# Attention output projection and memory-cell values run by token block, values ahead of queries and keys, one conditioning panel moved from TensorE to VectorE

## What is computed

```python
# first block, its attention layer
o = ...                                   # attention output, (T, 1024)
x = x + (o * silu(gate)) @ w_out_b        # "wo_b"

# second block, first layer (memory cell, "mlstm")
cond = silu(c)
ada = cond @ ada_w[0] + ada_b[0]          # shift, scale, gate: six vectors of 1024
h = rmsnorm(x, norm_g[0, 0]) * (1 + sc1) + sh1
proj = h @ w_in                           # q (512), k (512), v (1024), i, f gates (8 + 8), output gate og (1024)
hh = mlstm_chunkwise(q, k, v, i_pre, f_pre)   # 8 heads
y = (rmsnorm(hh, head_g) * sigmoid(og)) @ w_out
x = x + g1 * rmsnorm(y, norm_g[0, 1])
```

## Time and profile before

| | us |
|---|---|
| median of 3 runs | 1046.74 |
| lowest and highest | 1046.15, 1050.27 |
| the profiled execution, whole time | 1047.87 |
| its span in the trace | 1046.10 |
| PE busy in it | 993.2 (95%) |
| DVE busy | 752.1 (72%) |
| ACT busy | 525.6 (50%) |

### The profile page before, as it was taken

One profiled execution on the slowest core, in us unless ns is written; L12 is line 12 of the kernel. 1 busy time (PEld: TensorE's weight loads), 2 busy tenths in 40 slices (PEclk: granted clock), 3 DMA queues, 4 the chain that ended last, 5 costly groups with the idle time before them and its releaser, 6 DMA issues.

```text
span 1046.1 us, 19356 instructions
## 1 busy us (share of the span) xinstructions
PE 993.2 (95%) x8274; PEld 864.8 (83%) x8274; DVE 752.1 (72%) x1277; ACT 525.6 (50%) x798; POOL 36.4 (3%) x33
## 2 busy tenths in 40 slices
PE   5999999968999999999999999999999899999996
PEld 4788899967788888788867899999688788999995
DVE  6789889577889958646589665676587895664544
ACT  3358431316454677455366445454466855445442
POOL 0000044200000100000000000000000000000000
PEclk9999999999999999999999999999999999999999
DMA  9674410492456550564264477776646444476411
GB/s 379 248 284 161 162 43 4 162 389 100 154 211 219 221 242 11 232 242 161 81 242 161 170 294 303 287 291 264 240 164 215 188 161 161 172 296 256 171 72 41
DMA packets 15222, 205.40 MB, mean 196 GB/s; under 512 B 1816, under 2 KB 1816, under 8 KB 2976
## 3 DMA queue, kind: packets, MB, share of 16 engines
q1 hardware_dynamic: 14544, 202.55, 50.5%
q10 hardware_dynamic: 592, 1.61, 0.5%
HBM read 203.10 MB, written 1.05 MB: 195 GB/s over the span
## 4 chain that ended last, share of the span: by engine, by line
PE 83%; DVE 10%; ACT 3%; issue 2%; DMA 1%; SPq 0%; DVEq 0%; ACTq 0%
PE bank L455 20%; PE bank L457 20%; PE bank L456 20%; PE bank L758 5%; PE bank L404 4%; DVE slot_parts L2019 2%; PE bank L661 1%; PE bank L562 1%; DMA ring<-in_stream 1%; PE bank L739 1%; PE bank L634 1%; DMA pc<-in_params 1%; PE bank L623 1%; PE bank L900 1%; PE bank L537 1%
## 5 line engine op out<-in xcount | busy, mean ns | idle before, releaser
L455 PE MATMUL bank<-page_parts 128*128 128x512 f32 (+3 forms) x1222 | 428.8, 351 | 6.8 <-DVE page_parts L2301 2.2
L2019 DVE TENSOR_TENSOR slot_parts<-ring,page_parts 128x2048 fp32r<-128x2048 f32 (+2 forms) x117 | 261.4, 2251 | 53.4 <-ACT page_parts L1356 52.9
L457 PE MATMUL bank<-page_parts 128*128 128x512 f32 (+2 forms) x750 | 291.4, 389 | 0.0
L456 PE MATMUL bank<-slot_parts,page_parts 128*128 128x512 f32 (+2 forms) x750 | 290.9, 388 | 0.0
L455 PEld LDWEIGHTS bank<-page_parts 128*128 128x128 f32 x1222 | 232.3, 190 | 36.5 <-issue 3.7
L1356 ACT ACTIVATE page_parts<-ring 128x2048 fp32r<-128x2048 f32 (+2 forms) x121 | 225.0, 1884 | 52.6 <-PE bank L457 28.1
L457 PEld LDWEIGHTS bank<-page_parts 128*128 128x128 f32 x750 | 141.3, 188 | 29.0
L456 PEld LDWEIGHTS bank<-slot_parts,page_parts 128*128 128x128 f32 x750 | 141.8, 189 | 26.8
L1434 ACT ACTIVATE arena<-bank 128x512 f32<-128x512 f32 (+2 forms) x134 | 74.2, 575 | 127.2 <-PE bank L457 67.0
L457 PE MATMUL bank<-page_parts,slot_parts 128*128 128x256 f32 x472 | 133.6, 283 | 0.0
L456 PE MATMUL bank<-page_parts 128*128 128x256 f32 x472 | 133.6, 283 | 0.0
(11 more groups left out here) (318 smaller groups left out, 1114.2 us busy)
## 6 DMA issues: line engine op xcount, KB each, us to landing
ring<-in_stream SPq DMA_DIRECT2D x95, 2048.0 KB, 8.0
arena<-in_x SPq DMA_DIRECT2D x2, 512.0 KB, 4.3
arena<-in_gn ACTq DMA_DIRECT2D x2, 512.0 KB, 4.4
out<-arena SPq DMA_DIRECT2D x2, 512.0 KB, 2.6
cc<-in_consts SPq DMA_DIRECT2D x1, 899.0 KB, 6.6
small<-in_cond ACTq DMA_DIRECT2D x1, 512.0 KB, 10.1
pc<-in_params SPq DMA_DIRECT2D x1, 287.0 KB, 6.8
arena<-in_head_sel ACTq DMA_DIRECT2D x1, 32.0 KB
```

What stands on the lines that cost most here:

```text
L455: mm(out, a[0], b[0], start=start, stop=False)
L456: mm(out, a[0], b[1], start=False, stop=False)
L457: return mm(out, a[1], b[0], start=False, stop=stop)
L2019: tt(unit_parts(n)[1], lo, hi, ALU.subtract).then_inc(dv.step("w_lo"), 1)
```

## The change: what it does

`wo_b` and `v2` are done by `split_blocks`: both halves of the output for token block 0, then both for block 1, with the four units kept until their use in block 1. The transposes of `hT_c` go by token block too, into `wo_b`'s block 1 and `v2`'s block 0 (`turn_block`). Order on PE is `wo_b`, `v2`, gates, `spread(0)`, `q2`, `k2`. The conditioning panel 12 is no longer multiplied on PE; it is reserved with panel 13 (`ada(2)`) behind `k2` and summed on DVE, and on DVE the modulation and diagonal of the first gate come ahead of the `v2` splits. The panel order is now 31, 32 `wo_b`; 33, 34 `v2`; 35 `q2`; 36 `k2`; 37, 38 conditioning; 39, 40 `og`. Units keep their pages by rotation: `wo_b` 28 to 31 on 15, 16, 3, 10; `v2` 32 to 35 on 6, 14, 1, 2; `q2` 36, 37 on 11, 15; `k2` 38, 39 again on 11, 15, because `from_first` is called anew for each panel; `og` 40 to 43 on 13, 15, 16, 8 as before.

```diff
 # PE
-            for half in range(2):
-                split_tok(("wo_b", half), split_parts(O1_PAGES), first_of(15, 16, 3), wait=("o1T_split", 0) if half == 0 else None)
+            def beside_wo_b(tb, n):
+
+                if (tb, n) == (1, 2):
+                    turn_block("hT_c", XN, 0, lambda g: (sem("xn"), 5))
+
+            def beside_v2(tb, n):
+
+                if (tb, n) == (0, 2):
+                    turn_block("hT_c", XN, 1, lambda g: (sem("xn"), 6))
...
+            split_blocks("wo_b", split_parts(O1_PAGES), from_first(15, 16, 3, 10), lambda tb, k: (sem("o1T_split"), k // 2 + 1), beside_wo_b)
...
-            ada_direct()
-            pe.wait_ge(sem("xn"), 6)
-            transposes("hT_c", XN)
-            ada_turned()
             stage[0] = "mlstm"
-            for name in ("q2", "k2"):
-                split_T((name,), split_parts(MLSTM_PAGES), first_of(6, 14, 11), wait=("hT_c_split", 0) if name == "q2" else None)
-                if name == "q2":
-                    ada(1)
+            split_blocks("v2", split_parts(MLSTM_PAGES), from_first(6, 14, 1, 2), lambda tb, k: (sem("hT_c_split"), 2 * tb + k // 4 + 1),
+                         beside_v2)
...
-            for half in range(2):
-                split_tok(("v2", half), split_parts(MLSTM_PAGES), first_of(6, 14, 11))
+            for name in ("q2", "k2"):
+                split_T((name,), split_parts(MLSTM_PAGES), from_first(11, 15, 16))
+            ada(2)
...
-            pe.wait_ge(*evacuated(("v2", 1, 1)))
+            pe.wait_ge(*evacuated(("k2", 1)))
 # ACT
-            split(unit_of["q2", 0] + 1)
+            split(unit_of["v2", 0] + 1)
             warm_root()
-            x_squares("wo_b")
-            ada_direct()
-            mod_scaled("hT_c", 0, hT2)
-            ada_turned()
...
+            for tb in range(TB):
+                x_block("wo_b", tb)
+                split(unit_of["v2", 0] + 2 + tb)
...
+            for tb in range(TB):
+                for half in range(2):
+                    copy(V2[:, tb, 4 * half:4 * half + 4, 0:DV], ("v2", half, tb))
...
+            for i in range(2):
+                split(ahead(("q2", i)))
+                pair([d[:, 2 * i:2 * i + 2, :] for d in Q2T_OF], ("q2", i))
+            act_.wait_ge(sem("m_total"), 1)
+            act(em_row[0:8, :], mt_row[0:8, :], ACT.Exp, scale=-1.0).then_inc(ac.step("gate_rows"), 1)
+            page_used.update({13: finished(("hT_c", 1, 1)), 8: finished("gates")})
+            copy(K2T[:, 0:2, :], ("k2", 0))
+            split(unit_of["og", 0] + 1)
+            copy(K2T[:, 2:4, :], ("k2", 1))
+            split(unit_of["og", 1] + 1)
 # DVE
             split_output("wo_b", "o1T", O1_PAGES)
-            split(unit_of["q2", 0] + 1)
-            add_to_x("wo_b")
...
+            modulation(4, 6, ())
+            gate_diagonal(0)
+            u = unit_of["v2", 0]
+            split(u + 1)
+            for tb in range(TB):
+                add_to_x("wo_b", (tb,))
+                for q in range(2):
+                    split_quarter(u + 2 + tb, q)
+                norm_block(tb)
+                for q in range(2, 4):
+                    split_quarter(u + 2 + tb, q)
+                split_rows("hT_c", MLSTM_PAGES, 0, tb)
+            for _ in range(4):
                 next_unit(("q2", 0))
...
+            ada(4)
             dve.wait_ge(sem("gate_ln"), 1)
...
             V.memset(V2[:, :, :, DV:DV + 1], 1.0).then_inc(dv.step(), 1)
-            next_unit(("q2", 0))
-            next_unit(("q2", 0))
             gate_row(0)
+            ada(4)
             split(unit_of["og", 1] + 1)
             dve.wait_ge(*finished("gate_cols"))
```

More of the change, by code:

```diff
@@ L976, in _, with from_first @@
             stage[0] = "wo_b"
-            for half in range(2):
-                split_tok(("wo_b", half), split_parts(O1_PAGES), first_of(15, 16, 3), wait=("o1T_split", 0) if half == 0 else None)
+            def beside_wo_b(tb, n):
[4 more added lines that the diff above has]
+                    turn_block("hT_c", XN, 1, lambda g: (sem("xn"), 6))
+            def from_first(*pages):
+                n = len(units) % len(pages)
+                return pages[-n:] + pages[:-n] if n else pages
+            split_blocks("wo_b", split_parts(O1_PAGES), from_first(15, 16, 3, 10), lambda tb, k: (sem("o1T_split"), k // 2 + 1), beside_wo_b)
             def spread(i):
@@ L987, in spread @@
                     ins.then_inc(filled(("gb", i, half)), 1)
-            def from_first(*pages):
-                n = len(units) % len(pages)
-                return pages[-n:] + pages[:-n] if n else pages
             def mlp(l, branch, src, wait, beside):
@@ L1705, in _ @@
             split(unit_of["wo_b", 1] + 1)
-            def mod_scaled(name, which, dst):
-                act_.wait_ge(sem("mod"), which + 1)
-                scaled(name, dst, MODS[which][0], MODS[which][1])
             def mlp(l, branch):
@@ L1785, in _ @@
             act_.dma_start(head_sel[0:8, :], sel_d).then_inc(sem("head_sel"), 16)
-            page_used.update({6: finished(("o1T", 3)), 14: finished(("at1", "O", 3)), 11: finished(("wo_b", 1, 1))})
-            split(unit_of["q2", 0] + 1)
+            page_used.update({6: finished(("o1T", 3)), 14: finished(("at1", "O", 3)), 1: finished(("at1", "O", 3)), 2: (sem("o1"), 2),
+                              11: finished(("wo_b", 1, 1))})
+            split(unit_of["v2", 0] + 1)
             warm_root()
-            x_squares("wo_b")
-            ada_direct()
-            mod_scaled("hT_c", 0, hT2)
-            ada_turned()
[L1793 to L1797, removed]
+            for tb in range(TB):
+                x_block("wo_b", tb)
+                split(unit_of["v2", 0] + 2 + tb)
+                p, (scale, bias) = ("hT_c", tb, 0), MODS[0]
+                act_.wait_ge(sem("mod"), 1)
+                act_.wait_ge(*finished(p))
+                for j in range(4):
+                    act(hT2[:, j, tb * P:(tb + 1) * P], bank(p)[:, j * P:(j + 1) * P], ACT.Identity, scale=scale[:, j:j + 1],
+                        bias=bias[:, j:j + 1]).then_inc(ac.frees(p) if j == 3 else ac.step(), 1)
+            for tb in range(TB):
+                for half in range(2):
+                    copy(V2[:, tb, 4 * half:4 * half + 4, 0:DV], ("v2", half, tb))
             gb = par("gate_b")
@@ L2516, in post_norm_block, with split_rows @@
                 dve.wait_ge(*dv.last)
-            def mlp(l, branch):
[L2520 to L2537, removed]
+            def split_rows(turned, pages, modulated, tb):
+                t = slice(tb * P, (tb + 1) * P)
+                hi, lo = split_parts(pages)
+                scale, bias = MODS[modulated]
+                p = (turned, tb, 1)
+                dve.wait_ge(*finished(p))
+                for j in range(4, 8):
+                    ts(hT2[:, j, t], bank(p)[:, (j - 4) * P:(j - 3) * P], scale[:, j:j + 1], bias[:, j:j + 1], ALU.mult,
+                       ALU.add).then_inc(dv.frees(p) if j == 7 else dv.step(), 1)
+                for g in range(2):
+                    js = slice(4 * g, 4 * g + 4)
+                    dve.wait_ge(*evacuated((turned, tb, g)))
+                    V.tensor_copy(hi[:, js, t], hT2[:, js, t]).then_inc(dv.step(), 1)
+                    dve.wait_ge(*dv.last)
+                    tt(lo[:, js, t], hT2[:, js, t], hi[:, js, t].bitcast(F32), ALU.subtract).then_inc(dv.step(turned + "_split"), 1)
+            def mlp(l, branch):
+                first, turned, modulated = unit_of["up", l, 0], f"hT_m{l}", (1, 4)[l]
                 def low_rows(e, n, tb):
@@ L2551, in mlp @@
                     split_quarter(first + 2, q)
-                split_rows(0)
+                split_rows(turned, MLP_PAGES, modulated, 0)
                 post_norm_block(2 * l, branch, 1)
@@ L2558, in mlp @@
                     split_quarter(first + 3, q)
-                split_rows(1)
+                split_rows(turned, MLP_PAGES, modulated, 1)
                 split(first + 4)
@@ L2581, in mlp @@
                     split(unit_of["cq"] + 1)
[L2584 to L2587, removed]
-                next_unit(("q2", 0))
[L2589 to L2593, removed]
+            modulation(4, 6, ())
[11 more added lines that the diff above has]
+            for _ in range(4):
+                next_unit(("q2", 0))
+            ada(4)
             dve.wait_ge(sem("gate_ln"), 1)
```

## The result

The changed kernel takes 1066.2 us (median; 1065.12 to 1070.58) against 1046.65 of the kernel before: 1.0186 times as long, interval 1.0169 to 1.0202, which is 17.7 to 21.1 us more. The prediction said 1065 and a sum of 18.4 us. Of these, 20.7 lie between the first matmul of `wo_b` and the first of `wo_c`, the projection behind the heads; the other 2.0 lie outside what the change touches.

What follows compares the result with a forecast made beforehand. PE was taken as the bound, with 83% of the chain. 14.8 + 0.4 + 3.2 = 18.4 us on the profiled 1047.87 gave 1066.3, so 1065 for the median; forecast's range 1060 to 1070, 8 in 10 from 1056 to 1071.

Steps and rivals of the forecast that it cites:

- The saving: From wo_b's start to v2's end: 80.6 us before, 74.4 for the same matmuls and transposes, 6.2 us saved if nothing waited.
- First seam, block 0: First transposes of hT_c, in wo_b: PE stands 5.65 us for the norm, as DVE waits for ACT's split of unit 34.
- First seam, block 1: Second transposes of hT_c, in v2: PE stands 1.75 us for block 1's norm.
- Second seam: Between k2 and the heads: og's first matmul waits for DVE's gate-column copy, which frees bank 7; 14.8 us later.
- The second limit: At og's start: panel 40 loads into k2's slot, then ACT and DVE splits and the copy follow, ending at 501.6.
- Behind the heads: At wo_c: it claims bank 1, which ACT frees with its second conditioning row, 0.4 us later than the row before.
- The clock: Behind the two new long PE waits the granted clock falls, costing 1.6 us each, 3.2 us in all.
- The bound of 2 x 1.7: Upper bound on the clock time lost behind the two new long PE waits; the lower bound was 0.
- the 1 us named as a sign: Sign to look for: k2 should end 1 us later than v2 did in the kernel before.
- the exception: At the kernel's start the clock was taken as 1.00 behind a wait of 11.72 us, against the idle-throttling rule.
- The 22.7 us of DVE's queue: Work put behind q2's end on DVE, cited against the case that nothing waits (1040.5 us, chance 0.07).
- a clock that doesn't fall: Case within the forecast: the clock stays up behind the new waits, 1062 us; a quarter of the forecast's chance of 0.78.

Runs made afterwards that it cites:

- the kernel with both seams mended: Changed kernel with the waits before the heads mended, ACT's v2 splits ahead of the squares, and modulation and diagonal behind both blocks; 1043.39 us, 0.9948 of the kernel before.
- the first experiment: Changed kernel with ACT's splits of v2's last two units put ahead of the squares; 1063.06 us, ratio 1.0145 to the kernel before.
- the second experiment: Changed kernel with DVE's copy of the gate columns ahead of the second conditioning sum and og splits; 1062.3 us, ratio 1.0127 to the kernel before.
- the third: Changed kernel with k2's units on pages 16 and 11 instead of 11 and 15; 1067.77 us, ratio 1.0189 to the kernel before.
- the run with the panel alone: Kernel before with only conditioning panel 12 summed on DVE instead of multiplied on PE, bank claims kept; 1048.4 us, ratio 1.0006.
- filled waits: Changed kernel with 66 overwritten matmuls added in PE's waits at the first transposes and before the heads; 1065.33 us, ratio 1.0167 to the kernel before.
- the kernel with the second seam mended: Changed kernel with k2's pages, DVE's scans, gate-column copy, og's splits and k2's copies reordered around the heads' start; 1053.28 us, ratio 1.0041 to the kernel before.

## Why the prediction was right

- **The saving.** Forecast 6.2 us if nothing waits; the kernel with both seams mended has 6.17 at the first `og` matmul, and as a whole 3.3 to 7.4.
- **First seam, block 0.** Forecast 5.65 us of wait; the trace has 5.15. Counted from `wo_b`'s start, which lies 0.5 us later in this trace than the 405.6 of the forecast, the adds were forecast done at 15.6 us and the first transposes at 22.05; the trace has 15.3 and 21.7. DVE's wait for ACT's split: forecast 3.4, measured 3.47. Shown to be the cause by the first experiment.
- **First seam, block 1.** Forecast 1.75, measured 1.71.
- **Second seam.** Forecast 14.8 us later at the first `og` matmul. Measured 17.3 (99.77 less 82.48), of which the clock behind the first seam is 2.9; 14.4 are left. The single waits are 1.20, 4.30 and 7.22 us, forecast 2.1 (487.45 to 489.5), 4.2 and 7.5; the first is shorter because ACT did the table load ahead of its wait for DVE's scans, at 482.27, where I had put its 1.28 us behind them. That the bank holds `og` is shown by the second experiment; that the panel's load is the next limit and a quicker DVE gains 1 us, by the third (0.84 in its trace). The second limit, 501.6, was worked out with a landing of 8.0 us, not with the median of 8.5 that I named, which gives 502.1; the trace has 8.2 (490.24 to 498.47).
- **Behind the heads.** Forecast 0.4 for the bank of the conditioning row; `wo_c` starts 20.7 us later than before and the first `num` 20.2, so 0.5. PE stands 0.82 us there in the two kernels with the old bank claims and 1.35 to 1.40 in every kernel with the new ones. That it is the conditioning row's bank rests on the count of claims: the profile names no engine for the longer wait.
- **The clock.** The one term that was too small. I took 1.6 us for each of two falls, by the row of a wait of 2.87 us (the row itself gives 1.7). In the profiled execution the clock was at half for 5.7 and 6.2 us of work behind the two waits (windows above), which is 2.9 and 3.1 us. It stayed at half for longer behind these waits than behind that short one. The bound of 2 x 1.7 that I gave was too low for this execution. The clock is also why `k2` ended 3.4 us later than `v2` had, counted from `wo_b`'s start, and not the 1 us named as a sign.
- **By the page.** The Trainium skill's rule ("TensorE: Matmul & The Clock Gate", Part 1), that an idle TensorE is throttled, was borne out at the waits of 5.15, 4.59 and 2.01 us in these traces. The start of the kernel, which the prediction took for the exception, is none. I read the printed 1.00 and not the durations: behind the 11.72 us idle, 16 transposes take 3.65 us, as the 16 at half clock in the run with the panel alone (3.67) and not as the 1.96 at full clock. The clock records of this trace begin only at 15.68 us, and the view prints 1.00 where it has none.
- **A slip without effect.** The 22.7 us of DVE's queue run from the end of unit 39's split (480.0), not from `q2`'s end (475.85).

The row of the start, from the timeline of PE in the kernel before:

```profile
11.72 3.65 PE L562 MATMUL bank<-cc,arena 128*128 128x128 f32 x16 [11.72 <-DVE arena L1961]
```

So the lower bound of 0 for the clock rested on a row that was misread, and with it the only reason that the text gives for the quarter of the chance put on a clock that doesn't fall. The forecast itself took the other row.

The middle of the forecast owes something to luck. Up to `wo_c`'s start the profiled execution lost 20.7 us, 2.3 more than the sum of 18.4: the clock term was 2.8 too small and the waits were put 0.4 too long. The 2.0 us outside lie where the change touches nothing: 0.6 lie ahead of `wo_b`, 1.4 behind `wo_c`'s start, where the clock fell for 3.4 us at 798.8 in this execution and not in the one of the kernel before. The median came within 1.2 us of 1065 all the same: the other three executions, with a mean granted clock of 0.979 to 0.982 against 0.974, are 4.3 to 5.5 us shorter.

Left open: how much of the 19.5 us is clock in the median execution. The mean clocks say that it is less than in the profiled one, and not where. The filled waits give 4.1 us in one pair of traces and 2 us, with an interval that reaches 0, in the medians.

## What to carry to other kernels

Moving work earlier on one engine saves only what the others can follow: here the count of 6.2 us saved on PE was right, and two short queues, with the clock behind them, lost four times that (25.7 us). In a hand-ordered program look, for each item put in front of a long-awaited small one (a copy that frees a bank, a norm), at what that item itself waits for: a page still in use, a slot that is freed last, another engine's split. Ask for weights where they are needed, not before the loop that would hide them, and count bank claims anew after any change to a shared rotation.

## What was not expected of the hardware

- Matmuls that lie in a wait are not without use. Taking 3.65 us of them out of a wait that stayed let the granted clock fall to half, and 16 transposes took 3.67 instead of 1.96 us.
- The length of a single wait doesn't tell whether the clock falls: it fell behind 2.01 us (first experiment) and 1.94 us (filled waits), and not behind the 1.71 us of the changed kernel's second transposes; but neither did it behind waits of 2.87 and 3.08 us in the trace of the first experiment, further ahead. At `wo_c`'s first matmul, behind 1.35 us, it fell in the kernel with the second seam mended and not in the one with both mended (rows below; one execution each).
- Behind waits of 5.15 and 7.22 us, with PE at work throughout, the clock stayed at half for another 5.7 and 6.2 us; behind the wait of 2.01 it was at half for 3.4 us in all.
- A printed clock of 1.00 can mean that no record is there. The start of the kernel reads 1.00, and its transposes run at half speed (3.65 us against 1.96).

The timeline of PE and a window of the first experiment's kernel, then a window of the kernel with the second seam mended and one of the kernel with both mended, each around `wo_c`'s first matmul (at 542.22 and 534.50 us):

```profile
225.97 0.74 PE L838 MATMUL bank<-arena 64*64 64x64 f32 x19 [2.87 <-issue]
232.82 1.68 PE L813 MATMUL bank<-arena 64*64 64x64 f32 x51 [3.08 <-issue]
```

```profile
225.00:240.00 15.00, 8.45 (x271) 8.03 (x272) 5.61 (x11) 3.52 (x5) 0.00 (x0) 1.00 0.78 292
540.00:550.00 10.00, 8.65 (x40) 7.16 (x38) 9.90 (x10) 3.92 (x8) 0.00 (x0) 0.83 0.57 244
530.00:545.00 15.00, 12.63 (x69) 10.53 (x70) 12.21 (x15) 9.05 (x17) 0.00 (x0) 1.00 0.51 216
```
